# Order of a pair's six weight loads on the sync queue in the expert stage of a hybrid decoder step

## The chip, the cores and the metric

The kernel runs on one core of a Trainium2 chip. The metric is the device time of one execution in microseconds (us). The kernel before took 1697.02 us in the median of three runs (1693.51 to 1700.8). All data are float32.

## The reference, cut to what matters

One layer of a decoder for 256 prompt tokens and 8 sample tokens (264 rows, width 2048): a combined input projection, two kinds of attention (stick-breaking and forgetting, the samples over a paged cache of 2048 positions), an output projection with residual, and then a mixture of experts. The change lies in the last part. Each token goes to two of 32 experts; each expert is a SwiGLU of inner width 256:

```python
h = silu(einsum('td,edf->tef', u, w_gate)) * einsum('td,edf->tef', u, w_up)
h = h * comb[:, :, None]              # zero but for the token's two experts
f = einsum('tef,efd->td', h, w_down)  # gate, up: 2048x256 each; down: 256x2048, per expert
```

So every expert has three weight pieces of 2048 x 256 x 4 bytes (2048 KB), and all 96 pieces are read once from memory in each execution. The result is added to the residual, normalised a last time and written.

## The kernel before, in words

Up to its attention and output projection the kernel is untouched by the change. The expert stage (`experts`, lines 1558 to 1856) walks over the 32 experts in 16 pairs. The tokens of an expert are gathered into 64 slots, so that a pair fills the 128 partitions. There are six weight slots in SBUF, `ws[:, 0..5]`, each 2048 KB: slots 0, 1, 2 hold gate, up and down of the first expert of a pair, slots 3, 4, 5 those of the second. Each slot has a semaphore W[k] for "loaded".

TensorE does for pair n (`pair`, L1722): `gate_up(0)` (reads slots 0 and 1; 64 matmuls in two column halves, L1682 and L1684), `gate_up(1)` (slots 3 and 4), `turn_over(0)` (two transposes of the products, L1691), `tokens(n+1)` (16 transposes of the next pair's gathered rows `xg`, L1672), `turn_over(1)`, `down(0)` (slot 2, L1703), `down(1)` (slot 5). `gate_up` waits for its two slots to be loaded and reports on gu0 or gu1 when it is through; `down` waits for its own slot and for the activated products of VectorE and ScalarE, and reports on y0 or y1. In pair 0 there is more between these steps: the sample rows' residual, norm and routing (L1710, L1718, and on VectorE `sample_norm` and `sample_route`).

The sync queue (SP) does nothing in this stage but issue weight loads, in the order of its program. For pair n and slot k it waits until TensorE is through with what lay in that slot, and then issues one DMA of 2048 KB: slots 0 and 1 are free when gu0 has reached n (gate_up(0) of pair n-1 done), slot 2 when y0 has (down(0) done), slots 3 and 4 at gu1 (gate_up(1) done), slot 5 at y1 (down(1) done). A wait in front holds back all loads behind it, whether their own slot is free or not. The six loads of pair 0 are issued in the stage before, on the sync queue too (L725 to L727), and keep their order. Loads of experts beyond the 16 pairs (`extra_pairs`) happen only if an expert overflows its slots; in the profile each of the three kinds of piece is issued 32 times, so there are none.

GpSimd gathers token rows for pair n+2 with an indirect DMA (L1615) once the transposes of pair n+1 have read `xg`, and writes each expert's results with an indirect DMA (L1629) to `y_rows`. VectorE copies the gate/up products out of PSUM (L1839), multiplies (L1846) and copies expert 0's results (L1850); ScalarE does the activations (L1765), the copy of the token transposes (L1757) and expert 1's results (L1775).

After the stage all engines meet, `y_rows` is read back by the sync queue (L1875), summed with the residual, normalised and stored.

Of the kernel before, what the change touches and what calls it, by code (L numbers as in the profile page):

```python
# [143 lines left out]
def load_expert(eng, a, ws, W, s, e):  # L144

    k = s
    if k % 3 == 2:
        dst = ws[:, s, :].rearrange("p (j d) -> p j d", j=2)
        src = a["w_expert_down"][0].rearrange("e (j p) d -> e p j d", p=P)[bass.ds(e, 1)].rearrange("a p j d -> (a p) j d")
    else:  # L150
        dst = ws[:, s, :]
        w = a["w_expert_gate" if k % 3 == 0 else "w_expert_up"][0].rearrange("e (p c) f -> e p (c f)", p=P)
        src = w[bass.ds(e, 1)].rearrange("a p f -> (a p) f")
    eng.dma_start(dst, src).then_inc(W[s], 16)
# [1403 lines left out]
def experts(nc, ctx, ws, W, a, ident, iota, gcol, lastq, xT, xn, xgT, xg, wr, br, bank, sem, E, idx, dest, gates, extra,  # L1558
# [25 lines left out]
    def extra_pairs(eng, pair):  # L1584

        with eng.If(in_use(eng, 0) > 0):
            with eng.Fori(EXP_PAIRS, PAIRS) as n:
                with eng.If(in_use(eng, 2 * (n - EXP_PAIRS)) > 0):
                    pair(n)

    with nc.Block() as block:
        @block.sync
        def _(sp):
            def free(k, n):

                sp.wait_ge(E[f"gu{k // 3}"] if k % 3 < 2 else E[f"y{k // 3}"], n)

            with sp.Fori(1, EXP_PAIRS) as n:
                for k in range(6):
                    free(k, n)  # L1600
                    load_expert(sp, a, ws, W, k, 2 * n + k // 3)

            def pair(n):
                for blk_ in range(2):
                    e = sp.value_load(extra[0:1, 0, bass.ds((n - EXP_PAIRS) * 2 + blk_, 1)], min_val=0, max_val=NE - 1)
                    for k in range(3 * blk_, 3 * blk_ + 3):
                        free(k, n)
                        load_expert(sp, a, ws, W, k, e)

            extra_pairs(sp, pair)  # L1610
# [361 lines left out]
```

## Time and profile before

| | |
|---|---|
| median of 3 runs | 1697.02 us |
| the profiled execution | 1693.25 us |
| its span, first to last instruction | 1691.5 us |
| TensorE matmuls busy | 1299.3 us (77%) |
| VectorE busy | 678.5 us (40%) |
| data moved | 576.59 MB, mean 341 GB/s |
| mean granted TensorE clock | 0.864 of full |

The profile cuts the span into 40 slices of 42 us. The expert stage's first matmul starts at 1088.75 us and its last ends at 1647.18 us, so it fills about a third of the span, slices 26 to 38. Times of rows are microseconds from the start of the span. "Idle before" in a row is the time in which the engine did nothing ahead of that instruction, and the arrow names what ended it.

### The profile page before, as it was taken

How to read it: one execution, taken by the hardware profiler on the slowest of the kernel's cores; microseconds unless marked ns; L12 is line 12 of the kernel's file. 1: busy time of each engine (PE TensorE's matmuls, PEld its weight loads, DVE VectorE, ACT ScalarE, POOL GpSimd, SP SyncE). 2: the span in 40 equal slices, each digit the busy share in tenths (PEclk: the TensorE clock that was granted, in tenths of full speed). 3: DMA queues.
4: the chain of work that ended last, by engine and by line, in shares of the span. 5: the costliest groups of instructions: out<-in, count | busy, mean ns of one | idle time of the engine just before them, and what ended most of it. 6: DMA issues, size and time to landing. Idle time of an engine off the chain costs nothing. (4 is left out here: it accounts for less than half of the span.)

```text
span 1691.5 us, 24894 instructions
## 1 busy us (share of the span) xinstructions
PE 1299.3 (77%) x7991; PEld 816.7 (48%) x7992; DVE 678.5 (40%) x4789; ACT 230.3 (14%) x447; POOL 60.7 (4%) x100
## 2 busy tenths in 40 slices
PE   5999487888697979379997676676777577876771
PEld 3777355555465756237774222443444344433431
DVE  3005875756575757677446950020010000000015
ACT  1011011301212203020002111010011001100101
POOL 1000000000000000010000000000001000000000
PEclk9999789998898989679998767687899878888995
DMA  8453899999989999999997999959999999999954
GB/s 269 90 191 141 286 389 394 398 398 391 354 335 398 370 398 356 373 362 335 362 359 298 408 389 364 404 226 384 395 360 396 393 377 383 357 389 392 393 222 156
DMA packets 201805, 576.59 MB, mean 341 GB/s; under 512 B 28529, under 2 KB 116898, under 8 KB 183618
## 3 DMA queue, kind: packets, MB, share of 16 engines
q1 hardware_dynamic: 122144, 507.85, 76.8%
q10 hardware_dynamic: 75122, 58.46, 10.8%
q0 software_dynamic: 4432, 9.05, 1.7%
q8 instruction: 43, 0.70, 0.2%
q14 instruction: 64, 0.52, 0.1%
HBM read 568.68 MB, written 17.77 MB: 347 GB/s over the span
## 5 line engine op out<-in xcount | busy, mean ns | idle before, releaser
L119 DVE CUSTOM_DVE_ANT_0 ws<-ws,xgT 128x128 f32<-128x128 f32 x2048 | 441.8, 282 | 68.2 <-DMA ws<-in_cache_fox_k 29.4
L1682 PE MATMUL bank<-ws,xgT 128*64 128x256 f32 x1024 | 264.2, 423 | 127.5 <-DMA ws<-in_w_expert_up 123.9
L800 PE MATMUL bank<-xn,ws 128*128 128x264 f32 x1024 | 266.1, 417 | 53.3 <-DMA ws<-in_w_in 53.3
L800 PEld LDWEIGHTS bank<-xn,ws 128*128 128x128 f32 x1024 | 204.0, 205 | 140.2 <-DMA ws<-in_w_in 61.0
L1682 PEld LDWEIGHTS bank<-ws,xgT 128*64 128x64 f32 x1024 | 154.2, 154 | 236.0 <-DMA ws<-in_w_expert_up 121.1
L1684 PE MATMUL bank<-ws,xgT 128*64 128x256 f32 x1024 | 264.1, 423 | 0.0
L785 PE MATMUL bank<-ws,PR 128*32 128x512 f32 x1024 | 155.4, 688 | 35.5 <-DMA ws<-in_cache_fox_v 28.5
L1839 DVE COPY gu<-bank 128x256 f32<-128x256 f32 x32 | 13.6, 425 | 412.6 <-PE bank L1684 412.6
L119 DVE DVE_READ_ACCUMULATOR2_ANT Z<- 128x1 f32 x2048 | 159.6, 78 | 0.0
L1684 PEld LDWEIGHTS bank<-ws,xgT 128*64 128x64 f32 x1024 | 154.1, 154 | 0.0
L1703 PE MATMUL bank<-ws,hT 128*32 128x512 f32 x1024 | 115.9, 605 | 12.7 <-ACT xgT L1757 12.5
L900 PE MATMUL bank<-qo,ws 128*128 128x256 f32 x512 | 116.1, 385 | 7.8 <-DVE qo L1339 7.8
L409 PE MATMUL bank<-xn,ws 128*128 128x264 f32 x512 | 116.4, 389 | 0.0
L900 PEld LDWEIGHTS bank<-qo,ws 128*128 128x128 f32 x512 | 97.1, 192 | 31.3 <-issue 14.3
L409 PEld LDWEIGHTS bank<-xn,ws 128*128 128x128 f32 x512 | 97.7, 192 | 19.1 <-issue 2.5
L1703 PEld LDWEIGHTS bank<-ws,hT 128*32 128x32 f32 x1024 | 32.4, 112 | 85.4 <-issue 69.4
L785 PEld LDWEIGHTS bank<-ws,PR 128*32 128x32 f32 x1024 | 21.9, 114 | 86.0 <-DMA ws<-in_cache_fox_v 50.4
L1765 ACT ACTIVATE si<-bank 128x128 f32<-128x128 f32 x32 | 8.8, 277 | 356.0 <-PE bank L1691 356.0
L127 PE MATMUL bank<-xg,lastq 128*128 128x512 f32 x64 | 31.9, 645 | 23.0 <-POOL gates L734 22.4
L1850 DVE COPY ys<-bank 128x512 f32<-128x512 f32 x32 | 20.6, 686 | 56.4 <-PE bank L1703 56.4
L1063 ACT ACTIVATE blk<-bank 128x264 f32<-128x264 f32 (+1 forms) x40 | 16.4, 410 | 176.5 <-PE bank L800 109.9
L1629 POOL DMA_INDIRECT y_rows<-ys,dest x32 | 29.1, 910 | 164.9 <-DVE ys L1850 127.9
(372 smaller groups left out, 954.7 us busy)
## 6 DMA issues: line engine op xcount, KB each, us to landing
ws<-in_cache_sb_k SPq DMA_DIRECT2D x128, 512.0 KB, 8.2
ws<-in_cache_fox_k SPq DMA_DIRECT2D x128, 512.0 KB, 10.0
ws<-in_cache_sb_v SPq DMA_DIRECT2D x128, 512.0 KB, 7.2
ws<-in_cache_fox_v SPq DMA_DIRECT2D x128, 512.0 KB, 10.2
ws<-in_w_expert_gate SPq DMA_DIRECT2D x32, 2048.0 KB, 15.4
ws<-in_w_expert_up SPq DMA_DIRECT2D x32, 2048.0 KB, 17.3
ws<-in_w_expert_down SPq DMA_DIRECT2D x32, 2048.0 KB, 20.0
ws<-in_w_in ACTq DMA_DIRECT2D x16, 2048.0 KB, 31.7
```

What stands on the lines that cost most here:

```text
L119: ins = dve.tensor_tensor_reduce(k, k, qb[:, (g * H + h) * HD:(g * H + h + 1) * HD], 1.0, 0.0, ALU.mult, ALU.add, Z[:, n % 2, g, h, t:t + 1])
L127: mm = pe.matmul(banks[i][:, :], lastq[:, n:n + 1].to_broadcast([P, P]), qpart[:, i * 512:(i + 1) * 512], start=True, stop=True)
L409: mm = pe.matmul(bank[4 + (2 * n + m) % 4][:, 0:T], wq[:, n % 4, c, m * P:(m + 1) * P], xn[:, c, :], start=(c == 0), stop=(c == KC - 1))
L785: mm = pe.matmul(bank[0][r0:r0 + 32, :], PR[:, g, t, :], vring[:, u, g, half * 512:(half + 1) * 512], start=(t == 0), stop=(t == PAGES - 1))
L800: mm = pe.matmul(out[:, 0:T], w[:, c, m * P:(m + 1) * P], xn[:, c, :], start=(c == 0), stop=(c == KC - 1))
L900: mm = pe.matmul(bank[2 + m][:, 0:SEQ], lhs, qo[:, c, 0:SEQ], start=(c == 0), stop=(c == KC - 1))
L1063: nc.scalar.activation(out, src, ACT.Copy).then_inc(S[done], 1)
L1629: pool.indirect_dma_start(y_half, bass.IndirectOffsetOnAxis(ap=dest[0:rows, 2 * n + k:2 * n + k + 1], axis=0), ys[k][0:rows, :], None, bou ...
L1682: pe.matmul(bank[2 * k][0:SLOTS, 0:256], lhs, ws[:, wg, c * 256:(c + 1) * 256], start=(c == 0), stop=(c == KC - 1))
L1684: mm = pe.matmul(bank[2 * k][SLOTS:P, 0:256], lhs, ws[:, wu, c * 256:(c + 1) * 256], start=(c == 0), stop=(c == KC - 1))
L1703: mm = pe.matmul(bank[4 + 2 * k + dc][q * HALF:(q + 1) * HALF, :], hT[k][:, j, h0:h0 + HALF], ws[:, wd, d0:d0 + 512], start=(j == 0), stop ...
L1850: dve.tensor_copy(ys[0][:, i * 512:(i + 1) * 512], bank[4 + i][:, :]).then_inc(E["yc0"], 1)
```

## The change

In the loop over pairs 1 to 15 the sync queue visits the slots in the order 0, 1, 3, 4, 2, 5 in place of 0, 1, 2, 3, 4, 5. It now waits for gu0 (twice), gu1 (twice), y0 and y1, where it waited for gu0, gu0, y0, gu1, gu1, y1. No instruction is added or removed; the semaphores, the sizes, the pair 0 loads and the loads of extra pairs are the same.

```diff
             with sp.Fori(1, EXP_PAIRS) as n:
-                for k in range(6):
+                for k in (0, 1, 3, 4, 2, 5):
                     free(k, n)
                     load_expert(sp, a, ws, W, k, 2 * n + k // 3)
```

## Rows read from the trace of the kernel before

**Rows 1.** The page: data moved per slice of the span.
```profile
GB/s 269 90 191 141 286 389 394 398 398 391 354 335 398 370 398 356 373 362 335 362 359 298 408 389 364 404 226 384 395 360 396 393 377 383 357 389 392 393 222 156
```

**Rows 2.** Waits of TensorE, 1090 to 1691 us: total us, times, longest.
```profile
PE bank L1682 <- DMA ws<-in_w_expert_up: 123.9, 15, 9.2
```

**Rows 3.** Waits of the sync queue, 1180 to 1640 us.
```profile
SPq L154 <- PE bank L1703: 319.6, 26, 24.7
SPq L154 <- PE bank L1684: 75.7, 12, 6.3
```

**Rows 4.** Timeline of the sync queue: start us, us, what is issued.
```profile
1129.11 0.38 SPq L154 DMA_DIRECT2D ws<-in_w_expert_down  x1
...
1139.72 0.34 SPq L154 DMA_DIRECT2D ws<-in_w_expert_gate  x1
...
1231.83 0.38 SPq L154 DMA_DIRECT2D ws<-in_w_expert_down  x1
1232.41 0.70 SPq L154 DMA_DIRECT2D ws<-in_w_expert_gate  x1
1233.20 0.70 SPq L154 DMA_DIRECT2D ws<-in_w_expert_up  x1
1235.26 0.38 SPq L154 DMA_DIRECT2D ws<-in_w_expert_down  x1
...
1610.76 0.38 SPq L154 DMA_DIRECT2D ws<-in_w_expert_down  x1
```

**Rows 5.** The issues at 1232.41, 1233.20 and 1235.26 each: issue to landing.
```profile
DMA to landing us min/median/max: 13.2/13.2/13.2
DMA to landing us min/median/max: 17.1/17.1/17.1
DMA to landing us min/median/max: 20.0/20.0/20.0
```

**Rows 6.** Stretches: length; PE, PEld, DVE, ACT, POOL busy; clock, DMA share, GB/s.
```profile
1234.00:1236.00 2.00, 2.00 (x20) 0.76 (x14) 0.00 (x0) 0.65 (x2) 0.90 (x1) 1.00 1.00 401
...
1262.00:1264.00 2.00, 1.69 (x16) 0.55 (x20) 0.29 (x1) 0.42 (x2) 1.02 (x1) 1.00 0.62 262
1264.00:1266.00 2.00, 2.00 (x24) 0.65 (x20) 0.00 (x0) 0.00 (x0) 0.00 (x0) 1.00 0.49 111
1266.00:1268.00 2.00, 2.00 (x24) 0.60 (x20) 1.29 (x2) 0.00 (x0) 0.00 (x0) 1.00 0.66 205
```

**Rows 7.** The same view: the first and last fed stretch of 24 us, and 481 us.
```profile
1135.00:1159.00 24.00, 16.08 (x126) 10.44 (x122) 1.14 (x3) 1.58 (x4) 0.48 (x1) 0.79 1.01 428
...
1582.00:1606.00 24.00, 15.89 (x128) 10.23 (x125) 1.14 (x3) 1.18 (x3) 0.90 (x1) 0.86 1.01 428
...
1133.00:1614.00 481.00, 360.48 (x2966) 197.29 (x2962) 38.00 (x84) 47.62 (x112) 38.14 (x41) 0.87 0.93 381
```

**Rows 8.** Timeline of TensorE, 1255 to 1304 us.
```profile
1259.43 0.44 PE L1691 MATMUL bank<-ident,gu 128*128 128x128 f32 x2
...
1262.31 7.07 PE L1703 MATMUL bank<-ws,hT 128*32 128x512 f32 x64 [0.42 <-ACT xgT L1757]
1269.31 0.43 PE L1682 MATMUL bank<-ws,xgT 128*64 128x256 f32 x1
...
1276.06 0.38 PE L1684 MATMUL bank<-ws,xgT 128*64 128x256 f32 x1
1285.07 0.69 PE L1682 MATMUL bank<-ws,xgT 128*64 128x256 f32 x1 [8.63 <-DMA ws<-in_w_expert_up]
...
1293.86 0.44 PE L1691 MATMUL bank<-ident,gu 128*128 128x128 f32 x2
```

**Rows 9.** Stretches around a wait of TensorE, columns as in rows 6.
```profile
1142.50:1147.40 4.90, 0.00 (x0) 0.00 (x0) 0.00 (x0) 0.00 (x0) 0.00 (x0) 0.50 0.99 421
1147.40:1152.60 5.20, 5.15 (x28) 2.98 (x30) 0.00 (x0) 0.00 (x0) 0.00 (x0) 0.55 1.05 438
```

**Rows 10.** Indirect DMAs, 1130 to 1640 us: the gathers' landing, then the scatters'.
```profile
DMA to landing us min/median/max: 4.8/5.0/5.7
...
DMA to landing us min/median/max: 7.7/8.5/14.1
```

**Rows 11.** The stage's start: 20 us as in rows 6, then TensorE's timeline.
```profile
1110.00:1130.00 20.00, 13.31 (x152) 6.52 (x152) 8.32 (x43) 3.68 (x8) 0.95 (x1) 0.83 0.08 24
...
1112.41 1.21 PE L1718 MATMUL bank<-wr,xn 128*8 128x36 f32 x64
...
1132.40 0.43 PE L1682 MATMUL bank<-ws,xgT 128*64 128x256 f32 x1
```

**Rows 12.** The stage's end: timeline of TensorE.
```profile
1638.90 0.44 PE L1691 MATMUL bank<-ident,gu 128*128 128x128 f32 x2
...
1640.11 7.07 PE L1703 MATMUL bank<-ws,hT 128*32 128x512 f32 x64 [0.19 <-DVE hT L1846]
```

## The prediction

> **What bounds the kernel now.** I read the page's slices first, then the waits of the stage that the change touches, then the timelines of the two parties of those waits, and last the data rate in short stretches. The chain that ended last is of no use here: it reaches back only into the final norm.
>
> In slices 28 to 38, which lie wholly in the expert stage, the DMA engines move 357 to 396 GB/s, and TensorE has gaps [rows 1]. The only large wait of TensorE is for an "up" piece: 123.9 us in 15 waits, one for each of pairs 1 to 15 [rows 2]. So the stage waits for weights. The reader should now ask whether the DMA engines are always fed. They are not: the sync queue waits 319.6 us for down steps (L1703) and 75.7 us for gate/up steps (L1684) [rows 3], and in each period there are some 4 us in which it has issued nothing that is still to be moved. From 1262 to 1268 us the rate falls to 262, 111 and 205 GB/s [rows 6], while fed stretches of 24 us run at 428 to 431 (14 of them, mean 429), and the whole of 481 us at 381 [rows 7].
>
> The cause is a loop. At 1231.83 down(0) is through, and SP issues slot 2, then slots 3 and 4 at once, because gate_up(1) had been through long before: these two sat behind the wait for y0 [rows 4]. The engines run again at the full rate from 1234 [rows 6], some 2 us later. The three pieces behind the first land at 1245.6, 1250.3 and 1255.3 (issue plus 13.2, 17.1, 20.0) [rows 4, 5], about 4.9 us apart: one after the other, in the order of issue. On the slot 4 piece, 18.5 us after the first issue, gate_up(1) starts; up to the turn it takes 8.8 us, as it starts at the low clock (1285.07 to 1293.86), where a gate_up at the full clock takes 7.1 (1269.31 to 1276.44); then come the turn and the tokens (1259.43 to 1262.31, 2.9 us) and one of the two down steps (7.0 us for both, 3.5 for one) [rows 8]. 18.5 + 8.8 + 2.9 + 3.5 = 33.7 us and a few tenths to issue: this loop, and not the data rate, is the period, which from issue to issue is (1610.76 - 1129.11) / 14 = 34.40 us [rows 4]. 381 GB/s over 34.4 us is 13.1 MB a pair: six pieces of 2.097 MB (12.6) and 0.5 for the indirect DMAs. At 429 GB/s that takes 30.5 us, 5.09 a piece with its share of the rest [rows 7].
>
> **The change, part by part.** Slots 3 and 4 are now issued when gate_up(1) ends instead of after down(0): at 1259.4 [rows 8] where it is now near 1266.6, some 7 us earlier. Slot 2 moves behind them in the queue, but its own moment (down(0) done) stays, and slot 5 keeps its own; the next slots 0 and 1 stand behind y1, which is over before gate_up(0) ends. Nothing is added on SP: six issues a pair as before, 0.33 to 0.70 us each [rows 4].
>
> Steady state, with t = 0 where slot 1 lands and the engines always fed: slot 3 at 5.1, slot 4 at 10.2, slot 2 at 15.3, slot 5 at 20.4, slots 0 and 1 of the next pair at 25.4 and 30.5. TensorE: gate_up(0) 0 to 7.1, wait 3.1, gate_up(1) 10.2 to 17.3, turn and tokens to 20.2, down 20.2 to 27.2 (slot 2 there since 15.3, slot 5 is needed at 23.7 and there since 20.4), wait 3.3 [rows 8]. Slots 0 and 1 are free at 7.1 and their transfer's turn comes at 20.4; slots 3 and 4 at 17.3 against 30.5; slot 2 at 23.7 against 40.7; slot 5 at 27.2 against 45.8. With 2 us of start the closest has 11 us to spare. So the engines never run dry, and the period is the larger of 30.5 (data) and 24.1 (TensorE: 7.1 + 7.1 + 2.9 + 7.0). That is a gain of 34.4 - 30.5 = 3.9 us a pair. What is late next is the data itself: TensorE's wait of about 8.6 us turns into two of about 3.
>
> The stage's start. Today the engines do nearly nothing for 20 us (24 GB/s from 1110 to 1130), since slots 3 and 4 of pair 1 stand behind down(0) of pair 0 [rows 11]. gate_up(1) of pair 0 is over by 1112.4, so they now go out at about 1112.5 and have landed by 1125, in time that was empty. Slot 2 of pair 1 goes at 1129.1 as before, is on the rings at 1131.1 and is followed by slot 5: done at 1141.3, where today two pieces more are in front (10.2 us). Slots 0 and 1 of pair 2 are issued at 1139.7 [rows 4] (gate_up(0) of pair 1 starts at 1132.40 as before [rows 11]) and start at 1141.7, a hole of 0.4. From there all is fed: gate_up(1) of pair 1 needs no wait, and TensorE runs through to about 1157.
>
> From 1141.7 there are 14 pairs (2 to 15) x 30.5 = 427 us, which ends at 1568.7; pieces landed 0.9 us behind that count (1255.3 against 1234 + 4 x 5.09 = 1254.4) [rows 5, 6]. The last slot 5 piece is there at 1569.6.
>
> The stage's end. Slot 4 landed 10.2 us before it, so gate_up(1) ends 3.1 us before it at full clock and 1.4 later if it starts low [rows 8]; up to down(0) it takes 0.3 and 1.2 more (1638.90 to 1640.11 [rows 12]), and both downs 7.1: TensorE ends 5.5 to 6.9 us after the last landing; I take 6: 1575.6. Today it ends at 1640.11 + 7.07 = 1647.2 [rows 12]. All that follows (44.3 us) is the same work from the same state. The gain is 1647.2 - 1575.6 = 71.6 us: 54.6 in 14 periods, 9.8 at the start, about 7 at the end, where today gate_up(1), the turn and both downs follow a piece that is last but one.
>
> The profiled execution took 1693.25 us, 1.75 more than its span, and 3.8 less than the median. 1693.25 - 71.6 = 1621.7; at the median's level 1697.0 - 71.6 = 1625.4. I say 1625.
>
> Costs that the trace doesn't show. (a) The rate over 430 us without a pause: 429 from stretches of 24 us; slices of 42 us in the stages before often stop at 398 [rows 1]. At 398 a pair takes 32.9 us, 33.6 more in all: 1659. At 431 it is 2 us less. I take 429, since it is the same traffic (the same pieces, with the scatters among them), and keep both ends. (b) The gathers fall today into the dry 4 us and land in 5.0 us (5.7 at most); from now on they meet a full queue, as the scatters do today, with 8.5 (14.1 at most) [rows 10]. Their next use is a period later, some 27 us, so this costs nothing even at 14.1. (c) The clock. After the wait at 1139.5 the granted clock stood at 0.50 from 1142.5 on, and stayed so for 5.2 us of the work after it [rows 9], so it may fall in a wait of 3 us too. A gate_up that starts low takes 8.5 without its gap in place of 7.1 [rows 8]: 24.1 + 2 x 1.4 = 26.9, which the 30.5 of the data still cover. From below it costs nothing, from above see the rival.
>
> The Trainium skill, in DMA: Bandwidth & Descriptors (Specifications), gives about 358 GB/s as the limit of memory per core. By it a pair of 13.1 MB would take an estimated 36.6 us, and there would be nothing to gain but at the two ends. This case's trace disagrees with it for a core alone: 429 in 14 stretches, and even the mean with the dry gaps is 381 [rows 7].
>
> **The rivals.**
> 1. The data rate doesn't hold, or is shared worse when five transfers stand in the queue all the time. For it: no slice of the page shows more than 408 [rows 1]. Against it: five are outstanding today too when slots 0 and 1 have been issued (the three of [rows 5] are not all down by then), at 429 [rows 7]. Price: up to 33.6 us, 1659.
> 2. TensorE at the low clock becomes the bound. With 5.2 us more for each gate_up, twice a pair, if the low clock of [rows 9] held for all of it and past it, it takes at the most 24.1 + 10.4 = 34.5 us: the period stays and only the two ends gain (17 us): about 1680. For it: the low clock of [rows 9]. Against it: a TensorE that falls behind has no waits left in which the clock could fall.
> 3. Slower: the gather of the next pair's rows is pushed behind the weight queue. Its loop is landing + transposes + issue, landing plus about 3.2 us. If it has to sit out the five pieces in the queue (25.4) on top of its 5.0, that is 33.6 a pair, still below today's 34.4; behind six pieces 38.7, which is 14 x 4.3 = 60 more, less the 17 of the ends: about 1740. It decides from a landing of some 32 us on; the scatters, which meet the full queue today, land in 14.1 at most [rows 10]. The Trainium skill, in DMA: Bandwidth & Descriptors (Queues, rings and completion order), says that each DMA engine takes turns between the queues at the size of a packet, which speaks against this rival; the trace agrees for the scatters.
> 4. The change doesn't do what it says, because another wait holds slots 3 and 4 back: 1697. The order of the waits on SP leaves none that I can see.
>
> **How the numbers follow.** Forecast 0.83, rival 1 in its full size 0.07, rival 2 0.04, rival 3 0.03, no effect 0.03. The time is that of the forecast, 1625. Small errors of the forecast: 1% of the rate is 4 us, the clock at the end 2, the level of the runs 4; it alone is 1614 to 1637. The range reaches towards rival 1: 1611 to 1655. What a measurement here can tell from no change is 0.5%, 8.5 us. Faster by more than that: forecast, rivals 1 and 2 (1680 is 1% less), 0.94; within it 0.03; slower 0.03.
>
> **What would show it.** In the timeline of SP the issues of slots 3 and 4 come right after gate_up(1), and down pieces last; issues repeat every 30.5 us; stretches of 24 us and of 400 us both show about 429 GB/s, with no hole of 111; TensorE waits for "up" about 29 times for some 3 us; TensorE's last down ends near 1576, and 1110 to 1125 carries data. Wrong would be: a period over 31.5 with a fed queue (rate), waits for xgT or xg in TensorE (gather), or a period that TensorE fills at a clock near 0.5.

## The result and the profile after

The changed kernel took 1676.1 us in the median of five runs (1668.4 to 1677.9), beside 1694.9 for the kernel before (1688.7 to 1700.8): a ratio of 0.9895, 95% interval 0.9873 to 0.9918. A second comparison, on the chip of the last experiments, gave 0.9876 (0.9845 to 0.9907). So the change gains 1.1 to 1.2%, 19 to 20 us, where the prediction said 71.6 us. The time lies 21 us above the range given.

The profiled execution took 1668.4 us with a span of 1666.7, at the fast end of its runs; that of before took 1693.25. The expert stage, from its first matmul to the first read-back of `y_rows`, fell from 571.8 us (1088.75 to 1660.56) to 547.7 (1087.75 to 1635.49). Of the 24.8 us between the two executions, 24.1 lie in it.

The waits of TensorE from 1090 us to the end, which answer to [rows 2]:

```profile
PE bank L1682 <- DMA ws<-in_w_expert_up: 106.9, 27, 7.5
```

27 waits instead of 15, as forecast (29), but 4.0 us each and not 3. The timeline of the sync queue, to be held against [rows 4], shows one period:

```profile
1237.18 0.33 SPq L154 DMA_DIRECT2D ws<-in_w_expert_gate  x1
1237.60 0.38 SPq L154 DMA_DIRECT2D ws<-in_w_expert_up  x1
1243.51 3.82 SPq L154 DMA_DIRECT2D ws<-in_w_expert_down  x2
1260.81 0.35 SPq L154 DMA_DIRECT2D ws<-in_w_expert_gate  x1
1261.25 0.38 SPq L154 DMA_DIRECT2D ws<-in_w_expert_up  x1
1271.02 0.33 SPq L154 DMA_DIRECT2D ws<-in_w_expert_gate  x1
1271.44 0.38 SPq L154 DMA_DIRECT2D ws<-in_w_expert_up  x1
1277.35 3.82 SPq L154 DMA_DIRECT2D ws<-in_w_expert_down  x2
...
1589.45 3.82 SPq L154 DMA_DIRECT2D ws<-in_w_expert_down  x2
```

Slots 3 and 4 go out some 6 us before the first down piece, when gate_up(1) ends: the change does what it says. But from 1243.51 to 1589.45 are ten periods, 34.59 us each. The old order had 34.40. The 15 issues of the first down piece of a pair are 23.8, 28.9, 31.7 and then 34.9, 33.8, 34.8, 35.6, 34.4, 34.3, 35.0, 34.5, 34.6, 34.8, 34.2 us apart: the gain in the periods is made in the first three, and after that there is none. What the stage's end gives comes below, with the experiments.

The dry gaps are gone, and yet no more data moves. Queue by queue over ten periods of each kernel (q1 carries the weights, q0 the gathers and scatters; the last column is the time of their packets as a share of 16 engines over the stretch), first the kernel before, 1231.8 to 1576.6 us:

```profile
q1 hardware_dynamic: 11200, 125.83, 88.2%
q0 software_dynamic: 2661, 5.70, 5.2%
```

and the changed one, 1243.5 to 1589.5:

```profile
q1 hardware_dynamic: 11242, 126.49, 93.5%
q0 software_dynamic: 2656, 5.77, 5.1%
```

Per pair that is 0.882 x 34.48 = 30.4 us of weight packets before and 0.935 x 34.60 = 32.4 after, for the same bytes a pair; the gathers and scatters take 1.8 in both. The engines were idle 2.3 us a pair, and now 0.5; what they won there, the same weight packets now take longer. Short stretches (columns as in [rows 6]) show where:

```profile
1178.00:1186.00 8.00, 4.82 (x36) 2.13 (x30) 0.27 (x1) 1.08 (x2) 1.81 (x2) 0.83 1.01 426
1210.00:1217.00 7.00, 1.99 (x20) 0.39 (x12) 0.00 (x1) 1.08 (x2) 1.80 (x2) 1.00 0.98 265
1244.00:1252.00 8.00, 2.88 (x28) 0.65 (x20) 0.90 (x2) 1.08 (x2) 1.91 (x2) 0.97 1.00 419
1278.00:1286.00 8.00, 2.72 (x28) 0.61 (x20) 0.73 (x2) 1.08 (x2) 1.80 (x2) 0.98 1.01 296
1314.00:1321.00 7.00, 1.49 (x16) 0.26 (x8) 0.00 (x0) 1.08 (x2) 1.98 (x2) 0.91 0.98 301
```

The reader should compare the last two columns. In [rows 6] a low rate went with a low share: nothing was queued. Here the share stays at 0.98 to 1.01 and the rate falls to 265 to 301 all the same: the engines are occupied by packets that take longer. What is under way at these times is the gather of token rows (timeline of GpSimd):

```profile
1173.42 1.02 POOL L1615 DMA_INDIRECT xg<-u_rows,idx  x1 [19.01 <-PE bank L1672]
1205.23 0.95 POOL L1615 DMA_INDIRECT xg<-u_rows,idx  x1 [21.91 <-PE bank L1672]
1240.05 1.02 POOL L1615 DMA_INDIRECT xg<-u_rows,idx  x1 [24.70 <-PE bank L1672]
1273.97 0.97 POOL L1615 DMA_INDIRECT xg<-u_rows,idx  x1 [24.01 <-PE bank L1672]
1308.73 0.96 POOL L1615 DMA_INDIRECT xg<-u_rows,idx  x1 [24.96 <-PE bank L1672]
```

They land 11.0 to 12.2 us after their issue (5.0 before, [rows 10]):

```profile
DMA to landing us min/median/max: 11.0/11.4/12.2
```

The gathers of 1205, 1274 and 1309 have a slow stretch some 5 us behind them, those of 1173 and 1240 have none. These two are the gathers for pairs 4 and 6. Only pairs 4 and 6 have an expert with more than 24 prompt tokens (24 and 38; 33 and 30), and for those the kernel takes the branch that gathers 128 rows; all others gather 64. The trace agrees: these two instructions take 1.02 us and the others 0.95 to 0.97, and 62 and 63 rows of 8 KB arrive for them. That was the first hint that the form of the gather matters, and not its bytes: the gathers for the other pairs, from 2 on, fetch 11 to 41 rows.

The trace also records every DMA packet with its queue, size, start and duration. While the rows of a 64-row gather are on their way (some 5 us, from pair 5 on), the 16 KB weight packets take 0.90 to 1.10 us each in the mean; beside the two 128-row gathers they take 0.62, and undisturbed 0.611. The small gather for pair 3 (11 rows) gives 0.81. This also bears on the first three periods, which ran at 409 GB/s against 383 in the 11 behind them: only the gathers for pairs 3 and 4 fall into them, the smallest one and one of the 128-row form.

### The profile page after: what moved, and what is told of

Same layout as the page of the kernel before. It is cut to its first block and busy times, and to the rows that moved or that the text cites. A ratio compares the mean times of both kernels' runs of the same rounds, so it can differ in the third digit from the quotient of the medians.

```text
span 1666.7 us, 24894 instructions
## 1 busy us (share of the span) xinstructions
PE 1287.2 (77%) x7991; PEld 820.9 (49%) x7992; DVE 678.3 (41%) x4789; ACT 230.2 (14%) x447; POOL 60.7 (4%) x100
## 5 line engine op out<-in xcount | busy, mean ns | idle before, releaser
L119 DVE CUSTOM_DVE_ANT_0 ws<-ws,xgT 128x128 f32<-128x128 f32 x2048 | 441.6, 281 | 68.9 <-DMA ws<-in_cache_fox_k 31.4
L1682 PE MATMUL bank<-ws,xgT 128*64 128x256 f32 x1024 | 258.4, 417 | 110.5 <-DMA ws<-in_w_expert_up 106.9
L1684 PE MATMUL bank<-ws,xgT 128*64 128x256 f32 x1024 | 258.6, 417 | 0.0
L1682 PEld LDWEIGHTS bank<-ws,xgT 128*64 128x64 f32 x1024 | 151.8, 151 | 207.8 <-issue 123.9
L1684 PEld LDWEIGHTS bank<-ws,xgT 128*64 128x64 f32 x1024 | 151.6, 151 | 0.0
L900 PEld LDWEIGHTS bank<-qo,ws 128*128 128x128 f32 x512 | 97.4, 193 | 31.5 <-issue 14.3
L1703 PEld LDWEIGHTS bank<-ws,hT 128*32 128x32 f32 x1024 | 32.1, 111 | 84.3 <-issue 68.2
## 6 DMA issues: line engine op xcount, KB each, us to landing
ws<-in_w_expert_gate SPq DMA_DIRECT2D x32, 2048.0 KB, 17.6
ws<-in_w_in ACTq DMA_DIRECT2D x16, 2048.0 KB, 32.3
```

What stands on the lines that cost most here:

```text
L119: ins = dve.tensor_tensor_reduce(k, k, qb[:, (g * H + h) * HD:(g * H + h + 1) * HD], 1.0, 0.0, ALU.mult, ALU.add, Z[:, n % 2, g, h, t:t + 1])
L900: mm = pe.matmul(bank[2 + m][:, 0:SEQ], lhs, qo[:, c, 0:SEQ], start=(c == 0), stop=(c == KC - 1))
L1682: pe.matmul(bank[2 * k][0:SLOTS, 0:256], lhs, ws[:, wg, c * 256:(c + 1) * 256], start=(c == 0), stop=(c == KC - 1))
L1684: mm = pe.matmul(bank[2 * k][SLOTS:P, 0:256], lhs, ws[:, wu, c * 256:(c + 1) * 256], start=(c == 0), stop=(c == KC - 1))
L1703: mm = pe.matmul(bank[4 + 2 * k + dc][q * HALF:(q + 1) * HALF, :], hT[k][:, j, h0:h0 + HALF], ws[:, wd, d0:d0 + 512], start=(j == 0), stop ...
```

## The experiments

All edits are against the changed kernel unless the text says "old order"; times of kernels in one group are from one chip. Ratios are to the kernel before.

**Group 1: is it the gather?** Kernel before: 1690.9 us.

*All gathers over 128 rows (new order).* The unused rows are out of bounds and are skipped; the result is the same.

```diff
-                rest = pool.value_load(many2[0:1, n:n + 1], min_val=0, max_val=1)
                 wait_past(pool, E["xgp"], 4 * n)
-                with pool.If(rest > 0):
-                    gather(n, P)
-                with pool.Else():
-                    gather(n, SLOTS)
+                gather(n, P)
```

> The changed kernel, but every gather of token rows is issued over 128 rows instead of 64 or 128 (the rows past the first 64 are out of bounds in most pairs and are skipped, so the same bytes move). Theory G (the new order lets the 64-row gather run into a full weight queue, and there it slows all weight packets to about half speed for some 6 us): the stretches at 265 to 300 GB/s vanish as they are absent from the two 128-row gathers of the changed kernel's trace, 16 KB packets come down from 22.3 to about 19.8 us of engine time a pair, the period falls from 34.6 to about 32, the time to about 1676 - 14 x 2.3 = 1644. Rival Q (a full queue of five transfers is by itself slower, whatever the gather looks like): no change, 1676. Rival R (rows of real data matter, not the form): no change either, 1676.

Measured: 1655.8 us (1652.0 to 1657.6), ratio 0.9794 (0.9762 to 0.9825). The period is 33.2 us. Weights and indirect DMAs over ten periods (1240.1 to 1572.3), and the stretches behind the gathers of 1203.3, 1236.6 and 1270.4:

```profile
q1 hardware_dynamic: 11275, 126.96, 92.4%
q0 software_dynamic: 3232, 5.77, 4.5%
```

```profile
1208.00:1216.00 8.00, 2.54 (x26) 0.73 (x20) 0.23 (x1) 1.08 (x2) 1.80 (x2) 0.83 1.01 426
1242.00:1250.00 8.00, 2.54 (x22) 1.01 (x16) 0.00 (x0) 1.08 (x2) 1.91 (x2) 0.84 1.02 428
1275.00:1283.00 8.00, 2.52 (x26) 0.72 (x20) 0.36 (x1) 1.08 (x2) 1.81 (x2) 0.91 1.00 416
```

The slow stretches are gone, weight packets are back at 0.924 x 332.2 / 10 = 30.7 us a pair. In the packet records the 16 KB weight packets beside the gathers from pair 3 on take 0.61 to 0.63 us, with the same valid rows fetched. Theory G holds in kind; of the 32 us expected from the changed kernel 20 came, since the period stopped at 33.2 and not 32. (The changed kernel was not run on this chip; taken at its ratio, 0.9895, it would be at 1673, and the gain 17.) Rivals Q and R, which saw no change, are out. The edit takes out the branch as well, but the two 128-row gathers of the changed kernel had the branch and no slow stretch.

*Gathers of 16 rows (new order)*: `gather(n, 16)` in place of the branch; most token rows are left out.

> The changed kernel with gathers of 16 rows instead of 64 or 128, so most token rows are left out; everything else as it is. Theory G: the gather's own 0.9 us and the 2.6 us that it costs the weight packets go: period about 31.3, time about 1676 - 14 x 3.2 = 1631. Rival Q: only the gather's own packets go, 0.7 us a pair: 1666.

Measured: 1643.4 us (1639.3 to 1645.4), ratio 0.9709 (0.9675 to 0.9742), period 32.3. That is most of the gain expected by G (12 us short) and far beyond Q's 1666. Even 16 rows slow the weights a little: their packets take 31.4 us a pair here (97.2% of 323.5 us over ten), more than beside the 128-row gather.

*The same two edits in the old order.*

> The kernel before with gathers of 16 rows (most token rows left out). Theory G, and the loop that the prediction saw (period set by the wait for down(0), not by the data): the gather lies in the 4 us in which the weight queue is empty, so the period stays at 34.2 to 34.4 and the time at 1690 to 1695. Rival Q: the same. If instead the weights' start behind the gather matters, up to 1 us a pair: 1681.

> The kernel before with every gather issued over 128 rows. Theory G: the gather is in the empty 4 us, so nothing moves: 1690 to 1697. It would speak against G as the whole story if the old order gained as much from it as the new one.

Measured: 1691.1 us, ratio 1.0011 (0.9992 to 1.0030), and 1694.5 us, ratio 1.0020 (1.0002 to 1.0038). Neither gains anything. In the old order the period is not set by the data, and the gather lies in the gap that the loop leaves. The new order took the gap away, and with it the place where the gather was free.

**Group 2: which property of the gather, and where is the gain made?** Kernel before: 1690.2 us.

*A direct DMA of 0.26 MB over 64 partitions, and the same bytes over 128* (new order, one form of gather as above; the right rows are not fetched):

```diff
-                pool.indirect_dma_start(xg[0:rows, :], None, u_rows[0:SEQ, :], ...).then_inc(E["xg"], 16)
+                pool.dma_start(xg[0:64, 0:1024], u_rows[0:64, 0:1024]).then_inc(E["xg"], 16)   # first kernel
+                pool.dma_start(xg[:, 0:512], u_rows[0:P, 0:512]).then_inc(E["xg"], 16)         # second kernel
```

> The changed kernel with each gather replaced by a direct DMA on the same GpSimd queue, of 64 rows of 4 KB into partitions 0 to 63 (0.26 MB, about what the gather moves; the tokens are not the right ones, so the routing of rows is left out). 
Measured: 1650.6 us (ratio 0.9773, 0.9747 to 0.9800) and 1639.4 us (0.9710, 0.9685 to 0.9736). Ten periods of each, 33.0 and 32.1 us long; weights over 64 partitions first, then over 128:

```profile
q1 hardware_dynamic: 11313, 127.50, 95.5%
q0 software_dynamic: 2586, 5.70, 5.1%
```

```profile
q1 hardware_dynamic: 11343, 127.93, 95.1%
q0 software_dynamic: 2586, 5.70, 5.4%
```

Per pair 31.6 us of weight packets (of 330.5 us in all) against 30.5 (of 321.2). The stretches behind the transfers, two of each kernel, 64 partitions first:

```profile
1208.00:1216.00 8.00, 4.94 (x45) 1.57 (x38) 1.29 (x2) 1.08 (x2) 1.80 (x2) 0.96 1.01 356
1239.00:1247.00 8.00, 4.31 (x43) 1.03 (x32) 1.29 (x2) 1.09 (x2) 1.91 (x2) 0.95 1.00 336
```

```profile
1204.00:1212.00 8.00, 4.49 (x44) 1.35 (x38) 1.29 (x2) 1.08 (x2) 1.82 (x2) 0.94 1.02 428
1236.00:1244.00 8.00, 4.48 (x42) 1.49 (x36) 1.29 (x2) 1.08 (x2) 1.91 (x2) 0.86 1.01 425
```

The same bytes on the same queue cost the weights 1.1 us a pair more, and the kernel 11 us more, over 64 partitions than over 128, and the slow stretches stay only over 64. This difference is what theory P says, and theory I saw none. But P's time for the first kernel was wrong (1665 to 1676, period 34 to 34.6), and I's was right (1650, period 32.5; measured 33.0): the stretches are milder than those behind an indirect gather (336 to 357 GB/s against 265 to 301). The indirect 64-row gather costs the weights 1.9 us more (32.4) than the evenly spread DMA, so some part of it is the indirection or the rows themselves (8 KB each, or which rows). Yet over 128 rows the indirect gather costs next to nothing (30.7). Neither theory alone covers this; the two may act together, which no run separates.

*Gathers and scatters all over 128 rows* (new order).

> e1_wide (1655.8) with the scatters of results over 128 rows too. Theory P for the scatters as well: they come at a time when their packets meet the weights without slowing them in the trace, so little, 0 to 5 us better: 1651 to 1656. If the 64-row scatters were what keeps the period at 33.2 instead of 31: 1635.

Measured: 1679.6 us, ratio 0.9942 (0.9922 to 0.9962): 24 us slower than with wide gathers alone (group 1, ratio 0.9794). The expectation was wrong. Ten periods (1251.0 to 1599.2) show a third way to lose:

```profile
q1 hardware_dynamic: 11203, 125.88, 88.1%
q0 software_dynamic: 4320, 5.77, 4.5%
```

The weight packets are as quick as ever, 30.7 us a pair, but the engines are idle again for 7.4% of the time, 2.6 us a pair. In the packet records nearly every period has one or two dips of up to 5 us in which some 4 to 10 weight packets are in flight and not 16, and they end within 2 us of the issue of two more pieces (1231.9 to 1234.7 around the issues at 1233.31 and 1233.75, for example). So a part of the engines has run out of pieces while the rest still works on earlier ones, and SP can't issue more before TensorE is through with what it waits for.
*The new order for pair 1 alone* (old order otherwise).

```diff
+            for k in (0, 1, 3, 4, 2, 5):
+                free(k, 1)
+                load_expert(sp, a, ws, W, k, 2 + k // 3)
-            with sp.Fori(1, EXP_PAIRS) as n:
+            with sp.Fori(2, EXP_PAIRS) as n:
```

> The kernel before, with the new order for the loads of pair 1 only, the old one for pairs 2 to 15. The prediction's term for the stage's start says that two pieces are moved in an empty 20 us: 10 us less than before, 1681, with the old period of 34.4 from there on. The rival is that the old loop makes the later pairs wait again so that nothing stays: 1691.

Measured: 1678.7 us, ratio 0.9936 (0.9917 to 0.9954). The first down issues of pairs 1 and 2:

```profile
1127.96 3.81 SPq L154 DMA_DIRECT2D ws<-in_w_expert_down  x2
1151.80 0.38 SPq L154 DMA_DIRECT2D ws<-in_w_expert_down  x1
```

The first period takes 23.8 us in place of 34.2, 10.4 less, and the later ones about 34.2: the old loop neither gives this back nor adds to it. The term for the stage's start, 9.8 us, has come true, and the time is close to the 1681 expected.

**Group 3: the two ends together.** Kernel before: 1693.4 us.

*The new order for pair 15 alone; and for pairs 1 and 15, the old one between.*

```diff
-            with sp.Fori(1, EXP_PAIRS) as n:
+            with sp.Fori(1, EXP_PAIRS - 1) as n:            # second kernel: from 2, after pair 1 in the new order
                 for k in range(6):
                     ...
+            for k in (0, 1, 3, 4, 2, 5):
+                free(k, EXP_PAIRS - 1)
+                load_expert(sp, a, ws, W, k, 2 * (EXP_PAIRS - 1) + k // 3)
```

> The kernel before, with the new order for pair 15 alone, the last pair of the loop. The prediction's term for the stage's end says 7 us less: 1684, at a level of the kernel before of 1690 to 1691. Rival: the last pieces land at the same time in any order and TensorE's work after them is what counts, 0 to 3 us.

> The kernel before, with the new order for pairs 1 and 15 and the old one for the 13 pairs between. If the new order's loop has gained nothing in the steady state (34.6 us a pair against 34.4) and all of its gain is from the two ends, this is as fast as the changed kernel: about 0.989 to 0.990 of the kernel before, 1672. If the middle pairs do hold a part of the gain, it stays at 1680 or above.

Measured: pair 15 alone 1676.7 us, ratio 0.9889 (0.9862 to 0.9916); pairs 1 and 15 1670.5 us, 0.9865 (0.9832 to 0.9897); and beside them the changed kernel again:

> The changed kernel once more, on the same chip as the runs beside it, so that e10_first_and_last can be compared with it: 0.989 of the kernel before, 1672.

1673.4 us, 0.9876 (0.9845 to 0.9907). The kernel that changes only the two ends is as fast as the one that changes all 15 pairs. The timeline of the sync queue at the end, pair 15 alone in the new order:

```profile
1610.89 3.81 SPq L154 DMA_DIRECT2D ws<-in_w_expert_down  x2
1649.91 2.70 SPq L1878 DMA_DIRECT2D ws<-y_rows  x6
```

From the last issue (1614.3, the second of the two) to the read-back are 35.6 us; in the kernel before they are 46.4 (1614.19 to 1660.56). That is 10.8 us. In the kernel with both ends changed they are 35.6 as well, and its first period takes 23.8 us: 10.4 + 10.8 = 21.2 us by the timelines, where its median lies 22.9 below. In the changed kernel, where the queue is full and late, they are 42.6 (1592.89 to 1635.49), which leaves 3.8, and 44.4 in its second profiled execution, which leaves 1.9.

The medians are less exact than the timelines. Pair 15 alone is 17 to 19 us faster by them, but its profiled execution took 1682.6 us, just 10.8 below the median before, and the other three 1675.6 to 1677.0. One part that differs between executions is pair 0, from the first matmul to the end of down(0): 36.4 to 40.9 us in the profiled executions of the kernels in the old order, 35.6 to 40.8 in those in the new order. It takes longest where its granted clock is lowest (0.72 at 40.6 to 40.9 us, 0.81 at 36.4).

*The evenly spread direct DMA in the old order.*

> The kernel before with the evenly spread 0.26 MB direct DMA of e6_direct128 in place of each gather (tokens not the right ones). It is the control of e6: in the old order the period is set by the wait for down(0), so the form of the gather moves nothing, 1685 to 1692. If it gained here what it gained in the new order (37 us against the changed kernel), the cost of the gather would not be tied to the full queue.

Measured: 1692.6 us, ratio 0.9993 (0.9972 to 1.0014). What is worth some 30 us in the new order (ratio 0.9710 against 0.9876 and 0.9895) is worth nothing in the old one. This is the control for the kernels whose tokens are not the right ones: in the old order, wrong tokens as such change nothing.

## Why the prediction was wrong

**What bounds the kernel now: right.** A loop over the wait for down(0), not the data rate, sets the old period. Three changes of the gather left the old order where it was (ratios 1.0011, 1.0020, 0.9993), while the same three moved the new one by 17 to 31 us (ratios 0.9709, 0.9794 and 0.9710 against 0.9895).

**The moments of the issues, the landings' slack, the two short waits of TensorE: right** in kind. Slots 3 and 4 go out at the end of gate_up(1), the gathers land within 12.2 us (14.1 allowed) and nobody waits for them, and TensorE at a low clock did not become the bound (granted clock 0.90 over ten periods, and its waits for weights stay).

**The steady state: wrong, and this is nearly the whole error.** The prediction put the fed period at "30.5 us", "the larger of 30.5 (data) and 24.1 (TensorE)", and booked 54.6 us for 14 periods. Measured: 34.6 us, and -1.9 us over the 11 periods that are steady. The step that failed is the price of the data in (a) of the unknown costs: "I take 429, since it is the same traffic (the same pieces, with the scatters among them)". It was not the same traffic, because the gathers had been put at nothing in (b): "Their next use is a period later, some 27 us, so this costs nothing even at 14.1." That asked what a full queue does to the gather, and not what the gather does to a full queue. The rate of 429 GB/s had been read in stretches of 24 us that began 2 us or more behind the down steps, and so held the scatters but not one gather: all of those lay in the dry gaps. The rate was right for what it was measured on, and was carried over to a state with one more kind of traffic.

In engine time a pair, the forecast of 30.5 stands against 34.6 as follows. In the kernel before, weights (30.4) and indirect DMAs (1.8) already kept the engines busy for 32.2 us a pair, 1.7 more than 30.5. This stood in [rows 7]: a share of 0.93 over 34.4 us is 32.0 us of busy engines (some 31.5 if the 1.01 to 1.02 of the fed stretches counts as full), and the prediction used the rate of that row and not its share. In the dry gap too the share falls less than the rate: 0.59 and 193 GB/s from 1262 to 1268. After the change the weights need 32.4, which is 1.9 more, and 0.5 is idle: 1.7 + 1.9 + 0.5 = 4.1. The 1.9 come from the weight packets that the gathers slow: the gather over 128 rows took 1.7 of them back (30.7) and cost 0.5 more of idle, and the direct DMA over 128 partitions came to 32.1 us in all. The 30.5 were out of reach even then.

**Rival 1** ("the data rate doesn't hold, or is shared worse") was the right one, given 0.07. Its price was wrong: it was bounded by 398 GB/s, a figure of other stages, and the kernel came to 382 GB/s over ten periods. Nor is its cause, five weight loads in the queue, what did it: with the evenly spread DMA they stood there too, at 416 GB/s. A bound from other stages' traffic is no bound.

**The two ends: the start right, the end right only without a full queue.** The start was put at 9.8 us; the first period of the new order is 10.4 shorter, alone as in the changed kernel. The changed kernel's first three periods take 84.5 us against 102.7, 18.2 less; the prediction's terms make 9.8 + 2 x 3.9 = 17.6, so up to there it was right. In part that was luck: the gathers that fall into these periods are the two that slow the weights least. The end was put at 7; alone it is 10.8, behind a full queue 3.8. The stage of the profiled executions, 571.8 against 547.7, is then complete: 18.2 + 3.8 - 1.9 = 20.1 us from the change, and 4.0 from pair 0, ahead of the changed loads (40.4 us before, 36.4 after), which varies as much between executions of one order (see group 3). A kernel that changes the two ends alone gains as much: what the lead of the first periods brings in addition, the changed kernel loses again in the steady state and at its end.

**The Trainium skill's 358 GB/s** (DMA: Bandwidth & Descriptors, Specifications) is not what holds the period either: a core alone moved 416 GB/s over ten periods with the evenly spread DMA.

## What to carry to other kernels

A gap in which a queue runs dry may be the place where other transfers are free; before closing it, list what runs there, and take the rate for the new state from stretches that hold all kinds of traffic, or give the difference as a range. Set the DMA share times the period beside the bytes over the best rate: here they were 31.5 to 32.0 and 30.5 us before anything was changed, and the gap between them asks for a reason. When the rate falls while the DMA share stays at 1, look for a transfer of another shape in flight, and try it over the same 128 partitions as the bulk. The changed kernel with wide gathers beats both kernels: 0.9794 of the kernel before.

## What the runs showed of the hardware

- A gather of 64 rows of 8 KB (21 to 41 of them valid) beside a full weight queue lowered the rate from about 420 to 265 to 301 GB/s over stretches of 7 to 8 us, with the DMA share at 0.98 to 1.01; 16 KB weight packets took 0.90 to 1.10 us beside it in place of 0.611. A 128-row gather with the same valid rows left the rate at 416 to 428 and the packets at 0.61 to 0.63 us.
- Direct DMAs of 0.26 MB show the same in smaller: over 64 partitions weight packets take 31.6 us a pair and the rate behind the DMA falls to 336 to 357 GB/s; over 128 they take 30.5 and it stays at 419 to 428.
- Scatters over 128 rows in place of 64 cost 24 us in all, with no slower weight packet and 2.6 us of idle engines a pair, in dips with some 4 to 10 weight packets in flight. The cause is not shown by a test.
